# First modulation vectors by column blocks, on two engines, in one block with r, k and v; values centred while they are transposed

## The reference, cut to what matters

```python
mod_all = einsum('bd,lde->lbe', silu(c), ada_w) + ada_b          # per layer: 6 vectors of 2048
shift1, scale1, gate1, shift2, scale2, gate2 = split(mod_all[i], 6)
h = rmsnorm(x) * (1 + scale1) + shift1
dx = shift_by_one_token(h) - h
xr, xw, xk, xv, xa, xg = (h + dx * mu[i] for i in range(6))
r, k, v = xr @ w_rkv[0], xk @ w_rkv[1], xv @ w_rkv[2]
...                                                               # y: scan over tokens, per head of 64
S = S * w + sa * (kk * a) + v * k;   y = S @ r                    # linear in v
mean = mean(y); var = mean(square(y - mean))
y = (y - mean) * rsqrt(var + eps) * ln_w + ln_b
y = (y + sum(r * k * r_k) * v) * g
```

## Time and profile before

| | us |
|---|---|
| median of 3 runs | 2937.81 (2931.03 to 2937.84) |
| the profiled execution | 2924.65 |
| its span | 2923.0 |
| first product of r | 141.5 after the span's start |
| PE, DVE, ACT busy | 2676.2, 2008.9, 1319.2 |

### The profile page before, as it was taken

One profiled execution on the slowest core, in us unless ns is written; L12 is line 12 of the kernel. 1 busy time (PEld: TensorE's weight loads), 2 busy tenths in 40 slices (PEclk: granted clock), 3 DMA queues, 4 the chain that ended last, 5 costly groups with the idle time before them and its releaser, 6 DMA issues.

```text
span 2923.0 us, 55067 instructions
## 1 busy us (share of the span) xinstructions
PE 2676.2 (92%) x20605; PEld 2341.9 (80%) x20605; DVE 2008.9 (69%) x2597; ACT 1319.2 (45%) x2010; POOL 44.5 (2%) x88
## 2 busy tenths in 40 slices
PE   1299997989988999999999979988989999999998
PEld 0288886888877888888888868877878888888887
DVE  6678853788768777777777786654767755555556
ACT  1155554444444554444444444344445534444444
POOL 1000002000000000000000000000000000000000
PEclk6599999999989999999999989999989999999999
DMA  7669957443347778878788768632848855665553
GB/s 306 258 220 315 306 166 252 137 149 132 129 132 268 234 263 294 281 259 285 261 285 274 240 233 276 216 123 66 273 166 284 288 168 186 193 188 187 183 170 115
DMA packets 472654, 639.95 MB, mean 219 GB/s; under 512 B 21909, under 2 KB 427834, under 8 KB 451770
## 3 DMA queue, kind: packets, MB, share of 16 engines
q1 hardware_dynamic: 468666, 625.31, 64.0%
q0 software_dynamic: 3840, 12.59, 1.2%
HBM read 623.14 MB, written 14.68 MB: 218 GB/s over the span
## 4 chain that ended last, share of the span: by engine, by line
PE 62%; DVE 5%; issue 2%; ACT 2%; DVEq 0%; ACTq 0%
PE ps L1338 38%; PE ps L1339 19%; DVE wlo L1326 2%; PE ps L1385 1%; PE ps L1014 1%; PE ps L1005 1%; ACT whi L1321 1%; DVE ada_acc L1371 1%; DVE nt L133 1%; DVE act L146 0%; PE ps L1041 0%; PE ps L1582 0%; PE ps L1096 0%; DVE gsum L100 0%; DVE x L318 0%
## 5 line engine op out<-in xcount | busy, mean ns | idle before, releaser
L1338 PE MATMUL ps<-act,whi 128*128 128x512 f32 x3808 | 1349.4, 399 | 38.6 <-DVE act L146 16.7
L1326 DVE TENSOR_TENSOR wlo<-raw,whi 128x1024 fp32r<-128x1024 f32 (+1 forms) x768 | 901.7, 1192 | 496.7 <-ACT whi L1321 493.4
L1339 PE MATMUL ps<-act,wlo 128*128 128x256 f32 x3808 | 1071.5, 281 | 0.0
L1321 ACT ACTIVATE whi<-raw 128x1024 fp32r<-128x1024 f32 (+1 forms) x768 | 773.9, 1030 | 649.6 <-PE ps L1339 647.5
L1338 PEld LDWEIGHTS ps<-act,whi 128*128 128x128 f32 x3808 | 723.3, 190 | 214.1 <-DVE wlo L1326 23.7
L1338 PE MATMUL ps<-hid,whi 128*128 128x512 f32 x2176 | 776.9, 399 | 11.8 <-DVE wlo L1326 8.8
L1339 PEld LDWEIGHTS ps<-act,wlo 128*128 128x128 f32 x3808 | 727.1, 191 | 0.0
L1339 PE MATMUL ps<-hid,wlo 128*128 128x256 f32 x2176 | 616.5, 283 | 0.0
L1338 PEld LDWEIGHTS ps<-hid,whi 128*128 128x128 f32 x2176 | 414.7, 191 | 112.8 <-DVE wlo L1326 11.6
L1339 PEld LDWEIGHTS ps<-hid,wlo 128*128 128x128 f32 x2176 | 413.8, 190 | 0.0
L1371 DVE SCALAR_TENSOR_TENSOR ada_acc<-ada_ring,sc,ada_acc 128x2048 f32<-128x2048 f32 x128 | 300.3, 2346 | 0.3
(11 more groups left out here) (272 smaller groups left out, 2266.1 us busy)
## 6 DMA issues: line engine op xcount, KB each, us to landing
raw<-in_f_w SPq DMA_DIRECT2D x480, 512.0 KB, 4.6
ada_ring<-in_ada_w SPq DMA_DIRECT2D x172, 1024.0 KB, 7.4
raw<-in_a_w_rkv SPq DMA_DIRECT2D x96, 512.0 KB, 5.0
raw<-in_b_w_in SPq DMA_DIRECT2D x56, 512.0 KB, 4.0
raw<-in_f_w SPq DMA_DIRECT2D x64, 384.0 KB, 3.9
first_ring<-in_ada_w SPq DMA_DIRECT2D x20, 1024.0 KB, 5.3
raw<-in_a_w_o SPq DMA_DIRECT2D x32, 512.0 KB, 6.6
raw<-in_b_w_o SPq DMA_DIRECT2D x32, 512.0 KB, 6.0
```

Of the source, the lines that this page charges most:

```text
L1321: self.nc.scalar.activation(self.whi[:, u % SPL, 0:n], self.raw[:, u, 0:n], ACT.Copy).then_inc(self.s("hi_ready"), 1)
L1326: self.nc.vector.tensor_tensor(self.wlo[:, u % SPL, 0:n], self.raw[:, u, 0:n], self.whi[:, u % SPL, 0:n].bitcast(F32), SUB).then_inc(self. ...
L1338: self.nc.tensor.matmul(o, hi[:, kk, c0:c1], src[:, k].rearrange("p a t -> p (a t)"), start=k == 0, stop=False)
L1339: last = self.nc.tensor.matmul(o[:, T:2 * T], lo[:, kk, c0:c1], src[:, k, 0, :], start=False, stop=k == ktotal - 1)
```

## The change

Five things.

1. The head is a class `Prologue` and stands in one block with r, k, v, the low-rank products and the mixing; there is no barrier between them.
2. `ada_w` comes by column blocks: 32 units of 1 MB again, but each of 4 rows and 512 columns per partition. A quarter q of the columns has 8 units, shift and scale in turn. Even units (shift) are added by DVE, 4 operations of 512 columns; odd units (scale) are multiplied by PE itself, 16 products of one column each straight from the ring. After the quarter's last unit, PE sums DVE's part by 4 products into the same bank. Modulation and `Mixed` then run for the quarter's 4 tiles (`quarter_act`, `quarter_dve`).
3. The last two units are issued after the first four weight units of r, and PE takes the last one (and its sum) between the third and the fourth unit of r.
4. The squares of x are summed by PE tile by tile (16 products of 256 columns), not by DVE.
5. In the mixing, the values are transposed by a product with I - 1/64 (`centre64`) in place of I, so y comes out centred: `mean` and `centred` go. `ada_op` has one accumulator, and the sum 4 products.

```diff
+class Prologue:
+    slots = 6
+    bank = (7, 5, 4, 6)
+    units = [(q, piece, kk) for q in range(4) for kk in range(4) for piece in range(2)]
+    last = 2
...
+    def after_part(self, eng, n):
+        if n % 2 == 0:
+            eng.wait_ge(self.p.s("part_added"), 4 * (n // 2 + 1))
+        else:
+            eng.wait_ge(self.p.s("first_tensor"), 9 + n // 2 + 1 + 8 * (n >= 3) + 8 * (n >= 5))
...
+    def sync(self, sp):
...
+        for n, (q, piece, kk) in enumerate(self.units):
+            if n == len(self.units) - self.last:
+                for u in range(4):
+                    p.load_unit(sp, u, self.first_phase["source"](0, u))
+            if n >= self.slots:
+                self.after_part(sp, n - self.slots)
+            at = piece * D + q * 512
+            sp.dma_start(p.first_ring[n % self.slots].rearrange("p (k n) -> p k n", k=4),
+                         view[:, 4 * kk:4 * kk + 4, at:at + 512]).then_inc(s(f"first_loaded{n % self.slots}"), 16)
...
+    def add_part(self, dve, n):
...
+        for r in range(4):
+            at = p.first_ring[slot][:, r * 512:(r + 1) * 512]
+            scale = p.sc[:, 4 * kk + r:4 * kk + r + 1]
...
+                dve.wait_ge(s("part_added"), row + r)
+                nc.vector.scalar_tensor_tensor(acc, at, scale, acc, MUL, ADD).then_inc(s("part_added"), 1)
...
+    def part(self, pe, n):
...
+        if n % 8 == 1:
...
+            nc.tensor.matmul(p.ps[:, self.bank[q], 0:8], p.ones[:], p.zeros[:], start=True, stop=False, skip_group_check=True)
+        pe.wait_ge(s(f"first_loaded{slot}"), 16 * (n // self.slots + 1))
+        for r in range(4):
+            for m in range(4):
+                last = nc.tensor.matmul(p.ps[:, self.bank[q], 4 * piece + m:4 * piece + m + 1],
+                                        p.first_ring[slot][:, r * 512 + m * P:r * 512 + (m + 1) * P], p.sc[:, 4 * kk + r:4 * kk + r + 1],
+                                        start=False, stop=False, skip_group_check=True)
+        last.then_inc(s("first_tensor"), 1)
+        if n % 8 == 7:
+            self.after_part(pe, n - 1)
+            for m in range(4):
+                last = nc.tensor.matmul(p.ps[:, self.bank[q], m:m + 1], p.ada_acc[:, q * 512 + m * P:q * 512 + (m + 1) * P], p.ones[:, 0:1],
+                                        start=False, stop=True, skip_group_check=True)
+            last.then_inc(s("ada_summed"), 1)
...
+    def tensor(self, pe):
...
+        for n in range(1, len(self.units) - self.last, 2):
+            self.part(pe, n)
+            if n in (1, 3):
+                self.squares(pe, range(8) if n == 1 else range(8, KT))
...
@@ -560,6 +567,8 @@
+                    if self.arriving and g == 0 and q == 3 and starts:
+                        self.arriving.last_quarter_pe(pe)
...
@@ -1689,16 +1832,16 @@
-            if n < 2:
+            if n == 0:
                 wait(dve, "ada_summed", i + sums0)
             else:
-                dve.wait_ge(s("ada_row"), i * KT + (n - 1))
-            acc = self.ada_acc[:, h * W:(h + 1) * W]
+                dve.wait_ge(s("ada_row"), i * KT + n)
+            acc = self.ada_acc[:, 0:W]
...
-                if post:
-                    centred(i - 1)
...
-                for j in range(2) if post else ():
-                    at(pe, i - 1, "y0", j)
-                    mean(i - 1, j)
...
-                    turn4(j, 3, LEFT, chunks(R[j]["vb"][:]), self.ident64)
+                    turn4(j, 3, LEFT, chunks(R[j]["vb"][:]), self.centre64)
...
-                            for h in range(2):
-                                last = nc.tensor.matmul(ps[:, 3, T + m:T + m + 1], self.ada_acc[:, (MS * h + m) * P:(MS * h + m + 1) * P],
-                                                        self.ones[:, 0:1], start=h == 0, stop=h == 1)
+                            last = nc.tensor.matmul(ps[:, 3, T + m:T + m + 1], self.ada_acc[:, m * P:(m + 1) * P],
+                                                    self.ones[:, 0:1], start=True, stop=True)
```

More of the change, by code:

```diff
@@ L308, in act @@
         act.wait_ge(p.s("x_added"), i * 2 + (self.g0 + g + 1))
[L309 removed]
+        if not (isinstance(i, int) and i * 2 + self.q0 + g == 0):
+            act.wait_ge(p.s("square_added"), i * 2 + (self.q0 + g))
         p.nc.scalar.activation(p.tmp[:], p.x[:, bass.ds(i * 4 + 2 * g, 2), :], ACT.Square).then_inc(p.s("squared"), 1)
@@ L1192, in layout @@
         self.ident64, self.minus64, self.m_D = head("ident64"), head("minus64"), head("m_D")
+        self.centre64 = head("centre64")
         two = lambda name: place(name, [P, 2, HD])[0]
@@ L1971, in keys @@
                     tt("BF", R[j]["BF"][:], pairs_of(j, 1), bc_pairs(self.m_BF), MUL)
-            def centred(i):
-                for j in range(2):
-                    at(dve, i, "meanp", j)
-                    nc.vector.scalar_tensor_tensor(R[j]["yc"][:], bank(j, 0, RIGHT), -1.0 / HD, R[j]["y"][:], MUL, ADD).then_inc(s("yc"), 1)
             def normed(i):
@@ L2126, in pairs @@
                 return last
-            def mean(i, j):
-                nc.tensor.matmul(bank(j, 0, RIGHT), self.blk[:], R[j]["y"][:], start=True, stop=True).then_inc(s("meanp"), 1)
             def var(i, j):
@@ L2278, in tensor @@
             stage_C(L - 1, 1, True, False)
-            for j in range(2):
-                at(pe, L - 1, "y0", j)
-                mean(L - 1, j)
             for j in range(2):
```

466 lines of the change are left out of this document (264 added, 202 removed).

## The result

The changed kernel takes **2915.70 us** (median of 20 runs, 2899.78 to 2937.78) against 2933.91 for the kernel before (20 runs, 2920.31 to 2948.88): a ratio of 0.9941, with an interval of 0.9926 to 0.9956. It is 17 us faster. Its profiled execution took 2915.85, with a span of 2914.0.

The account below looks back on a forecast made before the run. It took DVE to bound the head, and PE and DVE by turns the mixing. Profiled 2924.65 + 6 (head) - 9 (mixing) = 2921.7; that -3 carried to the median gave 2934 us, range 2918 to 2950.

Parts of the forecast that it names:

- The clock in the odd units: Head: PE's clock stays at 0.50 under one-column products, about 6.9 us per odd unit from about 50 to 139 us.
- r's first product: End of PE's chain of odd units, squares, sums and clearings in the head: start at 139 us, before at 141.50.
- r's first units: Behind the head: three units in 11.2 us, part 31 and its sum, a bare chain, fourth unit ending at 166.4.
- the bare chain: Ahead of r's fourth unit: modulation 1.4 us, then four tiles through ACT and DVE 4.1, PE idle for 5.5.
- the mixing term, -9: Whole mixing: -1.2 us per iteration eight times and -1.8 at its end, taken as -9, bounds -17 and -3.
- the head's +6: Head up to the end of r's fourth unit: 166.4 against 160.65, a loss of 6 us, bounds 0 to +12.
- The sum's length: Mixing, stage C: 8 products instead of 16 halve PE's sum from 1.95 us, -0.97 per iteration, all on the path.
- The -0.2 for stage N: Mixing, per iteration: PE -1.0 without the mean, DVE +0.5 with chained adds; taken as -0.2, bounds -1.0 and +0.5.
- -1.8 at the end: End of the mixing: from mean to `var` 2.2 us, of which a hand-over and ACT's square stay, so -1.8.
- The mixing gives all of it: Rival: PE the only bound in the mixing, -2 per iteration and the tail, -17, head +6: 2927 us; chance 0.15.
- The clock comes up: Rival: clock rises in the head, odd units at 3.5 us, r starts at 96: 2889 us; chance 0.12.
- the head loses more: Rival: PE at 0.50 for the whole head, +12 to +14, 2949 us with the mixing at -3; chance 0.13.

Follow-up runs that it names:

- The head run alone: The changed kernel's new head with the mixing of the kernel before, against the kernel before: 2930.6 us, ratio 0.9999.

## Why the prediction was wrong, point by point

- **The clock in the odd units: right.** 0.50 with PE fully busy from 48 us on, 6.8 us per unit, no wait of PE for ring slots or for DVE's parts.
- **r's first product: 139 forecast, 131.96 measured.** Four sizes were too high. The squares took 5.8 and 6.3 us to the next unit (7 and 7.5), the second and third odd unit 4.8 and 3.6 (5.2 each), the first of the other twelve 6.0 and the rest 6.83 from start to start (6.96, which is the recorded length and holds 0.13 of overlap). The sums and clearings were right.
- **r's first units: right but for one term.** Three units in 11.0 (11.2), the part 3.5 (3.8), the bare chain 5.6 (5.5), the cold fourth unit 5.3 (5.1). The last sum took 1.03, not 1.75, because the clock was still up. End at 158.4, not 166.4: the head is -2.3 where +6 was forecast, outside its own bounds of 0 to +12. Of these 8 us, 7 are the sizes of the point before. The head run alone (0.998 to 1.0018, -6 to +5 us) leaves +6 just outside and -2.3 inside.
- **The step that failed is the mixing term, -9, and beside it the head's +6.** The mixing measured -17 (the mixing took 364.3 us in the mean of three profiles with the old code, 347.1 in the mean of the two of the changed kernel), at the bound that I had left to a rival. The sum's length was right (1.05 instead of 1.95 us), but its worth was not: I took its own time, -7.8, and four more products in it cost 17 (give or take 7). The -0.2 for stage N, where I set DVE's +0.5 against PE's -1.0, was wrong too: I charged the chained adds to the path at 1.15 us an iteration. Back to back they cost DVE 0.8 (1.53, 3.17 and 2.32 us where it was 1.41, 2.73 and 2.07), and taking the chain away gives nothing that can be told (two accumulators with eight products 2930.9, one accumulator with eight 2932.55). So the mean, at -0.2 an iteration and -1.8 at the end, was put at some 3 us, and putting it back cost 7 (give or take 6). My terms also add up to -11, not to the -9 that I took; the 2 us had no reason but caution.
- **How the miss is made up.** The head is 8 us off and the mixing 8 us, and the three runs that the forecast started from had a median 3.9 us above that of the twenty (2937.81 and 2933.91). That is 20 us against the 18.3 between 2934 and 2915.70, within the intervals. So the direction was right, but its small size came from a loss in the head that was not there.
- **What was missing in the sum of terms is the price that products have beyond their own time.** For sixteen against four it is the clock, shown by width alone. For eight against four the low clock differs by only 5 us (8 with two accumulators), and the remaining idle time, some 5 us in small pieces of which no one releaser stands out, is not settled. Nor is it settled how the gain of 17 divides between the sum and the mean.
- **One profile stood for the kernel.** The prediction carried a difference from one execution of before to the median; that execution was 9 us below the median of 2933.91, with the shortest mixing of the three that were profiled. This did not enter the terms, but it made the bounds look safer than they were: an old mixing of 359 to 370 us says how wide such a term is.
- **The rivals.** "The mixing gives all of it" (-17) has the measured size, and at -17 with the head at its measured -2 it gives 2919 against 2915.70. Its mechanism, PE as the only bound and each product at its own time, is half right: taking DVE's chained adds away gave nothing that can be told, but it has 8 us for the sum, where the runs show 17 (give or take 7). That the two meet at -17 is in part luck. "The clock comes up" and "the head loses more" did not happen.

## What to carry to other kernels

Where PE is nine tenths busy, price a removed product at its full time at least and treat DVE's extra latency as hidden until a run shows otherwise; but the next products removed from the same place can give nothing, as from four to one here. Count one-column products apart, since sixteen together cost the clock of the work behind them. Widening such products to equal columns that nobody reads cost nothing here and saved 22 us where sixteen stood together; where four stood together it changed nothing that can be told. Work that can be done by either engine is split by their prices at the clock that PE will really have, and the split is bounded by what the DMAs deliver and by how soon the other engine frees their slots.

## What the runs showed of the hardware

- Products of 128 x 128 weights with 1 or with 64 columns take the same time from start to start: 6.8 us for a unit of 16 at 0.50 in both heads, and 3.7 or less at 1.00. The recorded lengths differ (250 and 275 ns).
- The clock stayed at 0.50 from 48 to 132 us, 84 us of nearly nothing but one-column products without a gap, and through 80 us of 64-column ones, and yet 64 columns in place of one kept it at 1.00 in sums of sixteen amid dense work (low clock 31 us instead of 91).
- Pairs of 512- and 256-column products run at 0.347 or at 0.353 us, 2% apart, by execution and stretch, with the clock at 1.00 in both.
- The same code of the mixing differed by 11 us between executions (358.8 and 369.6, the latter with the new head), and the low clock with it (53 and 68 us); in one and the same program it was 358.8 and 364.6.
- Four operations of DVE on 512 columns took 2.73 us where each waited only for the one before the last, and 3.17 where each waited for the last.
